# A head's key transposes placed earlier in the hgrn stage, another order of conv's modulation, and work moved across four stage borders, in a three-block kernel on one core

## The reference

```python
def reference(x, c, ctx, c_ctx, ...):
    x = first_block(x, c, ctx, c_ctx, ...)      # hgrn2 mixer, then convolution mixer, final norm
    x = second_block(x, c_2, ...)               # gMLP + mLSTM + sparse attention, MLP, final norm
    return third_block(x, c_3, ...)             # gated delta rule + rwkv7, gated feed-forward, final norm

# first block, mixer 0 (16 heads of width 128, run forward and backward over time)
def step(state, inp):                           # _chunk_gla, chunkwise
    bcum = jnp.cumsum(gc, axis=-2)
    inter = einsum(qc * exp(bcum), state)
    scores = einsum(qc * exp(bcum - b_ref), kc * exp(b_ref - bcum))
    intra = einsum(where(mask, scores, 0.0), vc)
    new_state = exp(b_end) * state + einsum(kc * exp(b_end - bcum), vc)
    return new_state, inter + intra

# first block, mixer 1
shift, scale, gate = _ada(c, ada_w[i], ada_b[i])   # silu(c) @ w + b: the modulation
# ... depthwise convolution, layer norm, two projections

# ends of the second and the third block
x = rms_norm(x, g_final)
h = rms_norm_3(x, norm1_w[i]) * (1.0 + scale1) + shift1; p = h @ w_in[i]      # third block's first step
merged = sigmoid(gl_a) * y_a + sigmoid(gl_b) * y_b
x = x + gate1 * (merged @ w_out[i]);  x = x + gate2 * conv_glu(h, w_ffn_in[i], conv_ffn[i], w_ffn_out[i])
return rms_norm_3(x, norm_f_w)
```

## Time and profile before

| | us |
|---|---|
| runs of the kernel, device time | 3748.23, 3751.0, 3756.35 |
| median | 3751.0 |
| profiled execution, device time | 3755.11 |
| its span in the trace | 3753.4 |
| TensorE busy | 3484.1 (93%) |
| VectorE, ScalarE, GpSimd busy | 2054.9 (55%), 1325.7 (35%), 689.6 (18%) |
| mean granted TensorE clock | 0.962 |

### The profile page before, as it was taken

One profiled execution on the slowest core, in us unless ns is written; L12 is line 12 of the kernel. 1 busy time (PEld: TensorE's weight loads), 2 busy tenths in 40 slices (PEclk: granted clock), 3 DMA queues, 4 the chain that ended last, 5 costly groups with the idle time before them and its releaser, 6 DMA issues. The chain is left out here.

```text
span 3753.4 us, 57949 instructions
## 1 busy us (share of the span) xinstructions
PE 3484.1 (93%) x24695; PEld 2603.1 (69%) x24695; DVE 2054.9 (55%) x3227; ACT 1325.7 (35%) x2215; POOL 689.6 (18%) x354
## 2 busy tenths in 40 slices
PE   8999999998999999889999999998997878999998
PEld 5778787876644437556777567887676676878886
DVE  4147777775499975613144346332567575065422
ACT  4246666664101124423244324322442213233321
POOL 0000000001100000202122023443630002434442
PEclk9999999998999999999799999999998979999999
DMA  7622132224466550422121133331310002323332
GB/s 269 224 71 55 55 81 55 54 55 117 135 190 184 176 185 29 113 49 51 40 51 46 51 107 90 96 96 50 102 48 3 3 3 64 96 84 96 96 94 69
DMA packets 517591, 331.16 MB, mean 88 GB/s; under 512 B 31356, under 2 KB 493749, under 8 KB 517078
## 3 DMA queue, kind: packets, MB, share of 16 engines
q1 hardware_dynamic: 517334, 327.45, 30.0%
HBM read 316.93 MB, written 10.49 MB: 87 GB/s over the span
## 5 line engine op out<-in xcount | busy, mean ns | idle before, releaser
L3801 POOL TENSOR_TENSOR tl_wl<-tl_w,tl_wh 128x1024 fp32r<-128x1024 f32 (+1 forms) x104 | 246.1, 2367 | 682.4 <-ACT tl_wh L3914 682.2
L1571 DVE SCALAR_TENSOR_TENSOR conv_u<-cv_pad,vec,conv_u 128x512 f32<-128x512 f32 (+1 forms) x540 | 327.2, 685 | 0.0
L1394 PE MATMUL cv_bank<-hT,cv_w 128*128 128x512 f32 x704 | 313.8, 599 | 0.0
L1394 PEld LDWEIGHTS cv_bank<-hT,cv_w 128*128 128x128 f32 x704 | 130.1, 190 | 163.8 <-issue 163.8
L2601 POOL TENSOR_TENSOR mp_wl<-mp_w,mp_wh 128x1024 fp32r<-128x1024 f32 x72 | 173.5, 2412 | 318.7 <-ACT mp_wh L2675 318.7
L3914 ACT ACTIVATE tl_wh<-tl_w 128x1024 fp32r<-128x1024 f32 (+1 forms) x104 | 108.5, 1043 | 332.1 <-PE tl_bank L3838 329.9
L736 PE MATMUL hg_bank<-hg_hh,hg_wh 128*128 128x512 f32 x512 | 207.9, 406 | 4.6 <-PEq L201 4.6
L738 PE MATMUL hg_bank<-hg_hh,hg_wl 128*128 128x512 f32 x512 | 203.3, 397 | 0.0
L737 PE MATMUL hg_bank<-hg_hl,hg_wh 128*128 128x512 f32 x512 | 202.9, 396 | 0.0
L3836 PE MATMUL tl_bank<-tl_room,tl_wh 128*128 128x512 f32 x464 | 183.3, 395 | 11.7 <-POOL tl_wl L3801 10.9
L3838 PE MATMUL tl_bank<-tl_room,tl_wl 128*128 128x512 f32 x464 | 183.3, 395 | 0.0
(11 more groups left out here) (773 smaller groups left out, 8722.7 us busy)
## 6 DMA issues: line engine op xcount, KB each, us to landing
cv_ada<-in_w_ada_dram SPq DMA_DIRECT2D x48, 1024.0 KB, 7.6
hg_w<-in_hgrn_w_in_dram SPq DMA_DIRECT2D x64, 512.0 KB, 7.1
mp_w<-in_w_mlp_dram SPq DMA_DIRECT2D x64, 512.0 KB, 3.9
open_w<-in_ada_w_dram SPq DMA_DIRECT2D x12, 2048.0 KB, 9.4
cv_w<-in_conv_w_in_dram SPq DMA_DIRECT2D x44, 512.0 KB, 4.1
tl_w<-in_w_ffn_in_dram SPq DMA_DIRECT2D x44, 512.0 KB, 3.9
fr_w<-in_w_in_dram SPq DMA_DIRECT2D x26, 512.0 KB, 3.8
side_w<-in_w_in_dram SPq DMA_DIRECT2D x24, 512.0 KB, 4.0
```

The costliest lines, as they stand in the source:

```text
L1394: ins = pe.matmul(ps[n % RING][:, :], slot(n)[:, k * P:(k + 1) * P], K.hT[:, k, :], start=(k == 0), stop=(k == KD - 1))
L1571: ins = dve.scalar_tensor_tensor(o, x, by, o, ALU.mult, ALU.add)
L3801: pool.tensor_tensor(WL[u % SPLIT][:, 0:n, :], W[u % RAW][:, 0:n, :], WH[u % SPLIT][:, 0:n, :].bitcast(F32), ALU.subtract).then_inc(low, 1)
```

## The change

**hgrn.** The five transposes leave `recur` and become `turn_keys(d, h)`, which `project` calls in the middle of a group: the forward keys inside the ZB group over the tokens in EARLY, the backward keys inside the G group in LATE, each after the third k. The last head keeps its order. On ScalarE `early` is split into `forward_gate` and `backward_gate`, `turn(0)` and `exps(1)` stand between them, `turn(1)` stands inside `late` ahead of the reading of G, and each head has two more ACT_TABLE_LOADs (30 in all, 137 rows for 107). VectorE's `sums(1)` goes ahead of `finish`, and `weights_low` of G and of ZB go behind `recur(0)` and `recur(1)`.

**conv.** One unit ahead of the totals, none behind, five beside the squares.

**attention to mlp.** The attention stage's SyncE fetches the first three up weights into tiles that are free by then; mlp waits on their semaphore. mlp's SyncE first fetches front's first two weights (512 KB each) into half of hT, and then its own, from the third tile on.

**mlp to front.** The squares of xT, their sum (eight matmuls), logarithm and exponential are done at the end of mlp, each square behind the scaling of its k. front has no norm of its own; WL(0) and WL(1) are computed by VectorE instead of GpSimd.

**gated delta to tail.** The delta stage fetches tail's first four weights (2 MB), ScalarE copies WH(0), and GpSimd computes WL(0).

**tail and store.** The store stage is gone. tail's TensorE transposes xT by k behind its scaling, ScalarE copies the left half, VectorE the right, and eight DMAs of half a row write the output.

```diff
-                def project(h, groups, owed=None, square=None):
+                def project(h, groups, owed=None, square=None, keys=None):
...
                             if owed is not None and n == 0 and k == 2:
                                 states(*owed)
+                            if keys is not None and n == len(groups) // 2 and k == 2:
+                                turn_keys(*keys)
...
-                def recur(d, h):
-                    p = h % 2
+                def turn_keys(d, h):
...
                     ins.then_inc(tr_ok, 1)
+
+                def recur(d, h):
+                    p = h % 2
+                    first = 0 if d == 0 else 1
                     if d == 1:
...
-                project(1, EARLY)
+                project(1, EARLY, keys=(0, 0))
                 recur(0, 0)
-                project(1, LATE, owed=(0, 0))
+                project(1, LATE, owed=(0, 0), keys=(1, 0))
                 recur(1, 0)
                 for h in range(2, NH):
-                    project(h, EARLY, owed=(1, h - 2), square=h - 2)
+                    project(h, EARLY, owed=(1, h - 2), square=h - 2, keys=(0, h - 1))
                     recur(0, h - 1)
-                    project(h, LATE, owed=(0, h - 1))
+                    project(h, LATE, owed=(0, h - 1), keys=(1, h - 1))
                     recur(1, h - 1)
                 states(1, NH - 2)
                 mean_square(NH - 2)
...
-                def early(h):
+                def forward_gate(h):
                     evacuate(h, ZF, 0)
                     evacuate(h, ZF, 1)
                     weights_high(Q, h, done(h, ZF, 1))
+
+                def backward_gate(h):
                     evacuate(h, ZB, 0)
                     evacuate(h, ZB, 1)
...
+                    if h:
+                        turn(1, h - 1)
...
                     if h >= 2:
                         square(h - 2)
+                    log(1, h - 1)
+                    if h >= 2:
                         inverse_root(h - 2)
-                    log(1, h - 1)
-                    if h == NH:
-                        heads_high(0, 4)
                     if h < NH:
-                        early(h)
+                        forward_gate(h)
+                        turn(0, h - 1)
                         act.preload_act_table_set(LOG_EXP_SET)
-                    turn(0, h - 1)
-                    if h == NH:
-                        heads_high(4, 9)
-                    exps(1, h - 1)
-                    if h == NH:
-                        heads_high(9, HO_HIGH)
-                    if h < NH:
+                        exps(1, h - 1)
+                        backward_gate(h)
+                        act.preload_act_table_set(LOG_EXP_SET)
                         log(0, h)
                         late(h)
-                    turn(1, h - 1)
-                    if h < NH:
                         exps(0, h)
+                    else:
+                        heads_high(0, 4)
+                        turn(0, h - 1)
+                        heads_high(4, 9)
+                        exps(1, h - 1)
+                        heads_high(9, HO_HIGH)
+                        turn(1, h - 1)
...
                     products(0, h - 1)
                     gates(1, h - 1)
+                    sums(1, h - 1)
                     if h >= 2:
                         finish(h - 2)
-                    sums(1, h - 1)
                     weights_low(Q, h)
-                    weights_low(G, h)
                     gates(0, h)
                     recur(0, h - 1)
+                    weights_low(G, h)
                     products(1, h - 1)
                     sums(0, h)
                     if h + 1 < NH:
                         weights_low(ZF, h + 1)
-                        weights_low(ZB, h + 1)
                     else:
                         gates(1, h)
                     recur(1, h - 1)
+                    if h + 1 < NH:
+                        weights_low(ZB, h + 1)
...
-    ahead, behind, ending = (spread, spread + 1), (spread + 2,), (NA - 2, NA - 1)
-    beside = {4: spread + 3, 10: spread + 4, 15: spread + 5}
+    ahead, behind, ending = (spread,), (), (NA - 2, NA - 1)
+    beside = {2: spread + 1, 6: spread + 2, 10: spread + 3, 14: spread + 4, 15: spread + 5}
...
+                up = [K.inp[f"w_up_{x}_2"][0].rearrange("(k p) n -> p k n", p=P)[:, :, 0:P] for x in "abc"]
+                sp.wait_ge(low, NG - 1)
+                sp.dma_start(W[0][:, 0:4, :], up[0]).then_inc(K.up_in, 16)
+                sp.dma_start(W[0][:, 4:8, :], up[1]).then_inc(K.up_in, 16)
+                sp.wait_ge(low, NG)
+                sp.dma_start(W[1][:, 0:4, :], up[2]).then_inc(K.up_in, 16)
...
+                for n, w in enumerate(K.front_w):
+                    sp.dma_start(w, w_front[:, :, PB + n * P:PB + (n + 1) * P]).then_inc(K.front_in, 16)
+                for y in range(2, UPS):
                     i, rest = divmod(y, 2)
-                    if y >= RAW:
+                    if y >= RAW + 2:
...
+                for k in range(KD):
+                    pe.wait_ge(x_sq, k + 1)
+                    pe.matmul(SUM[0][:, :], K.ones[:, :], sq[:, k % 2, :], start=(k == 0), stop=(k == KD - 1)).then_inc(x_sum, 1)
...
+                for k in range(KD):
+                    act.wait_ge(normed, k + 1)
+                    if k >= 2:
+                        act.wait_ge(x_sum, k - 1)
+                    act.activation(sq[:, k % 2, :], K.xT[:, k, :], ACT.Square).then_inc(x_sq, 1)
+                act.wait_ge(x_sum, KD)
+                act.activation(K.root3[:, :], SUM[0][:, :], ACT.Ln, scale=1.0 / DM, bias=K.epsc[:, 0:1]).then_inc(x_ln, 1)
+                act.wait_ge(x_ln, 1)
+                act.activation(K.root3[:, :], K.root3[:, :], ACT.Exp, scale=-0.5).then_inc(x_ln, 1)
...
                 masks_begin(K, pool, wide, made, fixed)
-                weights_low(0)
-                weights_low(1)
                 masks_level(pool, wide, fixed, 0)
...
-                for k in range(KD):
-                    pe.wait_ge(squared, k + 1)
-                    pe.matmul(SUM[:, :], K.ones[:, :], sq[:, k % 2, :], start=(k == 0), stop=(k == KD - 1)).then_inc(sq_sum, 1)
...
-                dve.wait_ge(rstd_ok, 1)
                 scaled(0)
+                for u in range(2):
+                    dve.wait_ge(high, u + 1)
+                    dve.tensor_tensor(WL[u][:, :, :], raw(u), WH[u][:, :, :].bitcast(F32), ALU.subtract).then_inc(low, 1)
...
+                if ahead:
+                    first_w, first_h, first_l, w = ahead
+                    for u in range(4):
+                        sp.dma_start(first_w[u][:, :, :], w[:, :, ZC + u * P:ZC + (u + 1) * P]).then_inc(K.tail_in, 16)
+                    sp.wait_ge(K.tail_in, 64)
+
+            if ahead:
+                @block.gpsimd
+                def _(pool):
+                    first_w, first_h, first_l, w = ahead
+                    pool.wait_ge(K.tail_high, 1)
+                    pool.tensor_tensor(first_l[:, :, :], first_w[0][:, :, :], first_h[:, :, :].bitcast(F32), ALU.subtract)
 
...
+                if ahead:
+                    first_w, first_h, first_l, w = ahead
+                    act.wait_ge(K.tail_in, 64)
+                    act.activation(first_h[:, :, :], first_w[0][:, :, :], ACT.Copy).then_inc(K.tail_high, 1)
...
-                    pool.wait_ge(high, u + 1)
+                    pool.wait_ge(high, u)
...
+                for k in range(KD):
+                    pe.wait_ge(t_ok, KD + k + 1)
+                    for e in range(TT):
+                        ins = pe.transpose(ps[TT * (k // 4) + e][:, (k % 4) * P:(k % 4 + 1) * P], K.xT[:, k, e * P:(e + 1) * P], K.ident[:, :])
+                    ins.then_inc(turned, 1)
...
-                for u in range(SPLIT - 1):
+                for u in range(1, SPLIT - 1):
...
+                act.wait_ge(turned, 4)
+                for e in range(TT):
+                    act.activation(o[:, e, 0:512], ps[e][:, :], ACT.Copy).then_inc(out_left, 1)
...
+                dve.wait_ge(turned, KD)
+                for e in range(TT):
+                    dve.tensor_copy(o[:, e, 512:DM], ps[TT + e][:, :]).then_inc(out_right, 1)
```

143 lines of the change are left out of this document (68 added, 75 removed).

## The result

The changed kernel takes 3691.4 us (median of four runs, 3685.7 to 3692.7) against 3753.7 for the kernel before on the same chip; the ratio is 0.9833, with a 95% interval of 0.9816 to 0.9850, so 1.7% faster. The forecast was 3690, range 3676 to 3710. The profiled execution has a span of 3689.0 us (3753.4 before).

The account below looks back on a forecast made before the run. TensorE, busy for 3484.1 of 3753.4 us, was taken as the bound, so time could come only from its idle 269 us. Terms -32 - 6 - 8.5 - 6 - 6 - 2.5 = -61 from 3751.0 gave 3690 us, range 3676 to 3710.

Parts of the forecast that it names:

- hgrn, what goes: hgrn: TensorE's 30 waits for ScalarE's key copies, 1.49 and 1.45 us per head, 42.5 us in all, vanish.
- (a): hgrn, TensorE: transposes interrupting a matmul group cost 0.15 us per head (0 to 0.3).
- (b): hgrn, behind the backward products: TensorE waits for the summed scores, 0.5 us per head (0.3 to 1.1).
- (c): hgrn, ScalarE: two more table loads per head, 1.28 us each, cost only if ScalarE's chain becomes late.
- The chain: hgrn: from ScalarE's reading of G to VectorE's backward products 33.5 us, TensorE's transposes at 35.0, slack 1.5 us.
- Rival D: hgrn: late products hold transposes and projection, period is chain plus 4.3 us; kernel slower from a 39.1 us chain; chance 0.02.
- conv: conv: one modulation unit ahead of the totals starts the squares' sum 8.1 us earlier; -6 us (-2 to -8).
- The doubt about late units: conv: modulation units' 1 MB of data might arrive late beside the squares, giving back what was won.
- the allowance: attention to mlp: second unit's weights queue behind 1 MB for front, +0.5 us as an estimate.
- The term for the norm: mlp to front: sums of squares start 6.1 us earlier, a barrier and table load add 1.8 us.
- The term for GpSimd's subtraction: mlp to front: first two scalings no longer slowed beside GpSimd's subtraction, 2.1 us back; VectorE's two subtractions fit beside ScalarE.
- gated delta to tail: Tail's start 8.0 us earlier with WL(0) at hand, 2.0 us lost to GpSimd's subtraction; -6 us (-4 to -8).

Follow-up runs that it names:

- e3: The kernel before with only TensorE's new order in hgrn, ScalarE and VectorE in the old order: 3788.5 us (1.0098).
- e9: The kernel before with only ScalarE's and VectorE's new orders in hgrn, TensorE as before: 3800.6 us (1.0129).
- e8: The changed kernel with the products of the summed scores moved into the next head's first projection group: 3686.9 us (0.9823).
- e5: The changed kernel with two more table loads per head in ScalarE's hgrn loop: 3715.3 us (0.9894).
- e4: The changed kernel with ScalarE's gate block in one piece again, without the two added table loads per head: 3703.4 us (0.9868).
- e1: The kernel before with the new hgrn stage alone, every other stage as before: 3719.7 us (0.9913).
- e7: The changed kernel with the first up weights fetched at mlp's start again, ahead of front's weights: 3702.0 us (0.9861).
- e10: The changed kernel with the norm of front's input behind the barrier again: 3699.9 us (0.9859).
- e6: The changed kernel with the subtraction for tail's first weights made by VectorE in a pause instead of GpSimd: 3688.4 us (0.9825).

## Why the prediction was right, point by point

**hgrn, what goes (42.5 us).** Right, and for the reason given: the copies queued in ScalarE (e3: transposing early alone makes the wait 2.0 us; e9: ScalarE's and VectorE's new orders alone take the wait for the copies away, and other waits take its place).

**hgrn, what comes.** (a) The interrupted group: 0.15 us per head forecast. From start to start, the projections' matmuls take 4.7 us more over 14 heads and the transposes of L790 before (L792 after) 4.9 less; nothing is left. (b) The summed scores: 0.5 forecast; 0.31 idle in the trace, and the products ahead of the wait and behind it (L809, L814) take 3.7 us more over 14 heads, 0.27 per head, so 0.58; e8 has 0.56. (c) The two loads: free, as worked out, because of the slack; e5 shows where that ends. The steady loop gained a little more than forecast (the period 39.04 instead of 39.3), and the ends of the stage gave some back: the waits at the transposes there are 2.5 us longer.

**The chain.** 33.5 us forecast against 35.0, slack 1.5; 33.7 against 34.8 in the trace, slack 1.1, and 1.06 by e5. It was the thinnest step and held. Rival D's mechanism exists (e4 and e5 stall just so), and its formula fits: in e5 the chain of 33.7 + 2.56 plus D's 4.3 is a period of 40.6, and 40.54 was measured. Its point was not reached: e5's 2.56 us of lateness cost 24 us of the gain of 33.

**conv.** -6 forecast, -3.9 measured from stage to stage in the one pair of traces. The stretch that was argued about gave 5.5 (31.3 to 25.9 us), and the squares' sum starts 7.9 us earlier as seen from the unit ahead (8.1 forecast); ahead of that unit the stage is 1.5 us longer. The TensorE stretch of conv is 503.6 to 506.1 in the four traces with the old order (before, e1, e3, e9) and 499.3 to 500.9 in the nine with the new one, a difference of 5.3 by their means; the kernel before has the shortest of the four (the others 505.5 to 506.1), so the 1.5 belongs to the one pair of traces. No run has the conv order alone. The doubt about late units didn't come true.

**attention to mlp.** -9.0 by the prediction's sum, which takes 2.7 us for the eight matmuls where the rows give 6.48 - 3.60 = 2.9; -8.5 with the allowance for front's 1 MB. At the border itself the traces have -6.1 idle and -2.8 in the eight matmuls, 8.9; the other 0.5 of the -9.5 lies in the attention stage (265.6 and 265.1). 9.2 by e7. The allowance was not needed: no wait for the second unit.

**mlp to front.** -6.4 by the sum, rounded to -6; -6.8 measured, and the agreement is in part luck. The term for the norm, -6.1 + 1.8 = -4.3, is right (4.6 by e10). The term for GpSimd's subtraction, -2.1, is the step that was mis-sized: it brought 0.5 (e10), since VectorE's two subtractions do not fit beside ScalarE but stand in the chain for 2.45 us. What filled the sum again is 1.6 us in the body of mlp, between the second group of eight and the first scaling (486.6 to 485.0 us), which no term had.

**gated delta to tail.** -8.0 and +2.0 forecast, -7.9 for the border, 2.1 by the row at 2980.28, -5.7 in all. The prediction named a delta stage longer by more than 3 us as a sign that it was wrong, and the stage is 6.2 longer. By itself that looks like a term wrong by a factor of three; with mid's -4.0, and with the clock taken out over 13 traces (2.1 us, e6), it is not. The sign was badly chosen, not the term.

**tail and store.** -2.5 forecast, -2.4 measured; no run has this part alone.

**The sum.** -61 forecast, -64 between the two profiled spans, -62 between the medians. The 3.5 us that no term had are small differences in untouched stages (mlstm -2.1).
